# The second part's first norm is taken out of the start: its sums go behind the first head's token products, its scaling and shift beside the first group's queries

## The reference, cut to what matters

```python
mod = silu(c) @ w_ada + b_ada
sh1, sc1, g1, sh2, sc2, g2 = split(mod, 6)
hn = rmsnorm(x, norm1_w) * (1.0 + sc1) + sh1      # the "first norm"
proj = hn @ w_in                                  # q, k, v, gates, ...
...                                               # retention, RG-LRU, gates -> merged
x = x + g1 * (merged @ w_out)
hn2 = rmsnorm(x, norm2_w) * (1.0 + sc2) + sh2
x = x + g2 * peer(hn2, ...)                       # queries, top-k, experts gathered by token
y = rmsnorm(x, final_norm_w)
```

## Time and profile before

| | |
|---|---|
| median of 3 runs | 3748.63 us (3748.52 to 3752.19) |
| the profiled execution | 3746.89 us |
| its span, first to last instruction | 3745.1 us |
| PE busy | 3125.7 us (83%) |
| DVE busy | 2968.1 us (79%) |
| POOL busy | 1932.0 us (52%) |
| ACT busy | 1273.7 us (34%) |
| moved by DMA | 1126.16 MB |

### The profile page before, as it was taken

One profiled execution on the slowest core, in us unless ns is written; L12 is line 12 of the kernel. 1 busy time (PEld: TensorE's weight loads), 2 busy tenths in 40 slices (PEclk: granted clock), 3 DMA queues, 4 the chain that ended last, 5 costly groups with the idle time before them and its releaser, 6 DMA issues.

```text
span 3745.1 us, 56383 instructions
## 1 busy us (share of the span) xinstructions
PE 3125.7 (83%) x17498; PEld 2479.7 (66%) x17498; DVE 2968.1 (79%) x6226; ACT 1273.7 (34%) x2928; POOL 1932.0 (52%) x1504
## 2 busy tenths in 40 slices
PE   7999999989899999878999999899899999960100
PEld 4777776656666668767878788788777888850000
DVE  3444357998888877898899999899998876679898
ACT  3222211121222221686555555555545650000000
POOL 0000014444454553445667676667666756777676
PEclk9999999999999999999999999999999999985555
DMA  7444354666777787778999999999999999999998
GB/s 257 135 139 140 118 168 149 213 215 209 230 252 258 259 305 267 248 250 316 401 375 397 385 376 379 345 383 396 346 380 362 409 405 402 410 386 358 346 355 305
DMA packets 435094, 1126.16 MB, mean 301 GB/s; under 512 B 41856, under 2 KB 174336, under 8 KB 434944
## 3 DMA queue, kind: packets, MB, share of 16 engines
q0 software_dynamic: 204800, 745.10, 54.0%
q1 hardware_dynamic: 225376, 369.46, 27.9%
q10 hardware_dynamic: 4768, 9.96, 0.7%
HBM read 1098.29 MB, written 26.10 MB: 300 GB/s over the span
## 4 chain that ended last, share of the span: by engine, by line
PE 33%; DVE 24%; issue 15%; DMA 11%; POOL 3%; ACT 1%; DVEq 0%; ACTq 0%; POOLq 0%; SPq 0%
PE vacc L2264 12%; DVE rows L1679 9%; PE vacc L858 7%; DMA rows<-in_peer_u,eidx 7%; PE scat L2198 3%; POOL rows L1476 3%; PE vacc L829 3%; DVE oh1w L1758 2%; DMA rows<-in_peer_v,eidx 2%; DMA rows<-in_peer_v,g1T 2%; PE vacc L2178 1%; PE scat L2251 1%; DVE eidf L1571 1%; DVE htok L1689 1%; DVE hot L1665 1%
## 5 line engine op out<-in xcount | busy, mean ns | idle before, releaser
L1476 POOL DMA_INDIRECT rows<-in_peer_u,eidx x1088 | 1411.7, 1298 | 1070.1 <-DVE dots L1679 691.6
L1679 DVE CUSTOM_DVE_ANT_0 rows<-rows,htok 128x1024 f32<-128x1024 f32 x1088 | 1353.1, 1271 | 131.1 <-DMA rows<-in_peer_u,eidx 120.2
L2264 PE MATMUL vacc<-W,vbuf 128*128 (+1 forms) x6144 | 1427.9, 388 | 31.0 <-DMA vbuf<-in_peer_v 19.8
L2264 PEld LDWEIGHTS vacc<-W,vbuf 128*128 128x128 f32 x6144 | 1158.3, 193 | 182.4 <-issue 32.5
L2013 ACT ACTIVATE oh<-iota,e2s 128x128 bf16<-128x128 f32 x1536 | 486.5, 391 | 17.2 <-DVE wpart L1729 10.1
L858 PE MATMUL vacc<-W 128*128 128x384 f32 x1280 | 436.5, 497 | 1.2 <-ACTq L759 1.2
L1460 POOL TENSOR_TENSOR hot<-hot,cid 128x864 f32<-128x864 f32 x68 | 129.3, 1906 | 585.8 <-DVE hot L1665 584.6
L1689 DVE SCALAR_TENSOR_TENSOR htok<-rows,dots,htok 128x1024 f32<-128x1024 f32 x256 | 328.9, 1285 | 39.8 <-DMA rows<-in_peer_v,eidx 32.4
L858 PEld LDWEIGHTS vacc<-W 128*128 128x128 f32 x1280 | 243.5, 194 | 169.0 <-issue 10.8
L1476 POOL DMA_INDIRECT rows<-in_peer_v,eidx x256 | 286.8, 1120 | 100.4 <-issue 78.6
L2020 ACT ACTIVATE W<-scat 128x256 f32 (+1 forms) x320 | 122.6, 383 | 583.9 <-PE scat L2251 515.2
(11 more groups left out here) (327 smaller groups left out, 3089.4 us busy)
## 6 DMA issues: line engine op xcount, KB each, us to landing
vbuf<-in_peer_v SPq DMA_DIRECT2D x384, 512.0 KB
W<-in_w_in SPq DMA_DIRECT2D x80, 512.0 KB, 6.8
W<-in_wq SPq DMA_DIRECT2D x64, 512.0 KB
vbuf<-in_w_ada SPq DMA_DIRECT2D x9, 2048.0 KB, 8.2
rows<-in_peer_u,eidx POOLq DMA_INDIRECT x1088
W<-in_w_in SPq DMA_DIRECT2D x16, 1024.0 KB, 5.7
W<-in_w_ada SPq DMA_DIRECT2D x3, 2048.0 KB, 15.9
W<-in_w_out SPq DMA_DIRECT2D x12, 512.0 KB, 8.3
```

The lines of the kernel that those rows point to most:

```text
L1476: g.indirect_dma_start(rows[:, s, :], None, table[:, :], bass.IndirectOffsetOnAxis(ap=picked, axis=0)).then_inc(landed[s], 16)
L1679: v.tensor_tensor_reduce(rows[:, s, :], rows[:, s, :], htok[:, at % 2, :], 1.0, 0.0, ALU.mult, ALU.add, dots_of(t)[:, c:c + 1]).then_inc(u ...
L2264: mm = pe.matmul(vacc[:, k, :], vbuf[:, s, k * P:(k + 1) * P], W[:, e1, :].rearrange("p o t -> p (o t)"), start=(clear and s == 0 and k % ...
```

## The change

It does the following.

- SP's order in block 1: the load of B's `x` goes from behind the second slab to behind the eleven small tables, and the tables go from the end to just behind `w_qkv`. `wab`, the five `w_part`, S0 and the late slab come after these. The list of loads is the same.
- B's squares, sums and roots leave block 1. In block 2 ACT does the squares after `tokens_low` of the first head and then the two roots; PE does the sums after `qkv_low` of the first head, before `mix_tensor`.
- The inversion of `rstdB` goes from DVE's start of block 2 to its end, where also the shift's columns are copied to a new tile `sh1`.
- The 8 scalings of `hnB` go to DVE in block 3, behind `scale(0)`.
- The 8 shifts of `hnB` go to ACT in block 3, into the hook of `cross(0)`: one after each query copy from the ninth to the sixteenth. Each adds to a new semaphore `hnB_ready`, and PE waits for all 8 before B's first token products.
- The semaphore `fold_ready` is merged into `ones_ready`.

```diff
@@ block 1, SP
                 ada_load(1)
-                sp.dma_start(hnB, I["xT"][:, TA:T]...).then_inc(x_in[1], 16)
                 ada_load(2)
                 ada_load(3)
                 w_in_load(sp, 0, 0)
+                sp.wait_ge(act_done, 1)
+                for dst, src in ((rope_c, "rope_c"), (rope_s, "rope_s"), (dmask, "dmask"), (smask, "smask"), (xi, "xi"),
+                                 (zeta, "zeta"), (szeta, "szeta"), (gch, "gch"), (h0, "h0"), (c0, "c0"), (iota, "iota")):
+                    sp.dma_start(dst[:], I[src]).then_inc(small_in, 16)
+                sp.dma_start(hnB, I["xT"][:, TA:T]...).then_inc(x_in[1], 16)
                 sp.wait_ge(ones_ready, 4)
                 wab_load(sp, 0)
                 for j in range(1, 6):
                     w_in_load(sp, 0, j)
-                sp.wait_ge(act_done, 1)
-                for dst, src in (the same eleven):
-                    sp.dma_start(dst[:], I[src]).then_inc(small_in, 16)
                 s0_load(sp, 0)
                 sp.wait_ge(mod_ps, len(EARLY))
                 slab_load(sp, 0)
@@ block 1, ACT
                 copy_row(0)
                 copy_row(1)
-                squares(hnB, LATER, KC)
-                act.wait_ge(ssum_ready, 2)
-                act.activation(rstdB[:, 0:CUT], nps[:, 0:CUT], ACT.Sqrt, ...).then_inc(sd_ready, 1)
-                act.activation(rstdB[:, CUT:LATER], tps[:, 0:CUT], ACT.Sqrt, ...).then_inc(sd_ready, 1)
                 copy_row(2)
                 copy_row(3)
@@ block 1, PE
                 turn(1)
-                sums(zB, KC)
                 slab(2)
@@ block 2, ACT
                 act.wait_ge(small_in, 240)
-                for k in range(KC):
-                    act.wait_ge(scaled, KC + k + 1)
-                    act.activation(hnB[:, k, :], hnB[:, k, :], ACT.Identity, bias=modT[:, SH1 + k, 0:1])
                 tokens_high(act, zA, 0)
                 tokens_low(act, zA, 0)
+                squares(act, hnB, LATER, KC)
+                act.wait_ge(ssum_ready, 2)
+                act.activation(rstdB[:, 0:CUT], nps[:, 0:CUT], ACT.Sqrt, ...).then_inc(sd_ready, 1)
+                act.activation(rstdB[:, CUT:LATER], tps[:, 0:CUT], ACT.Sqrt, ...).then_inc(sd_ready, 1)
@@ block 2, PE
                 qkv_low(pe, zA, 0)
+                sums(pe, zB, KC)
                 with pe.Fori(0, H - 1) as f:
                     mix_tensor(pe, zA, f, False)
@@ block 2, DVE
-                v.wait_ge(sd_ready, 3)
-                dl_(v.reciprocal(rstdB, rstdB))
-                for k in range(KC):
-                    v.scalar_tensor_tensor(hnB[:, k, :], hnB[:, k, :], gain[:, k, 0:1], rstdB, ALU.mult, ALU.mult).then_inc(scaled, 1)
...
                 dl_.end(H)
+                v.wait_ge(sd_ready, 3)
+                dl_(v.reciprocal(rstdB, rstdB))
+                v.tensor_copy(sh1[:, :], modT[:, SH1:SH1 + KC, 0])
                 v.wait_ge(st_free, zA.nst * H)
@@ block 3, DVE
                 scale(0)
+                for k in range(KC):
+                    v.scalar_tensor_tensor(hnB[:, k, :], hnB[:, k, :], gain[:, k, 0:1], rstdB, ALU.mult, ALU.mult).then_inc(scaled, 1)
@@ block 3, ACT
-                cross(0, lambda x: None)
+                def second_half(x):
+
+                    if x >= KC:
+                        act.wait_ge(scaled, x + 1)
+                        act.activation(hnB[:, x - KC, :], hnB[:, x - KC, :], ACT.Identity, bias=sh1[:, x - KC:x - KC + 1]).then_inc(hnB_ready, 1)
+                cross(0, second_half)
@@ block 3, PE
                 pe.wait_ge(qh_ready, 16)
+                pe.wait_ge(hnB_ready, KC)
                 qkv_high(pe, zB, 0)
```

More of the change, by code:

```diff
@@ L366, in program @@
         ada_in = [sem(f"ada_in{i}") for i in range(len(EARLY))]
-        scaled = sem("scaled")
+        scaled, hnB_ready = sem("scaled"), sem("hnB_ready")
         def w_in_load(sp, f, j):
@@ L417, in slab_columns, with squares, sums @@
             return mm
+        def squares(act, x, n, lo):
+            act.wait_ge(x_in[lo // KC], 16)
+            for k in range(KC):
+                if lo + k >= 2:
+                    act.wait_ge(sq_used, lo + k - 1)
+                act.activation(sq[k % 2][:, 0:n], x[:, k, 0:n], ACT.Square).then_inc(sq_ready, 1)
+        def sums(pe, z, lo):
+            for k in range(KC):
+                pe.wait_ge(sq_ready, lo + k + 1)
+                for n, (a, b) in enumerate(z.slices):
+                    dst = pslice(z, pj, n) if z.sample else (nps, tps)[n][:, 0:CUT]
+                    mm = pe.matmul(dst, ones[:, :], sq[k % 2][:, a:b], start=(k == 0), stop=(k == KC - 1))
+                mm.then_inc(sq_used, 1)
+            pe.wait_ge(sq_used, lo + KC)
+            pe.sem_inc(ssum_ready, 1)
         with nc.Block() as block:
@@ L470, in copy_row @@
                     act.activation(row[u], R[u][0:ROWS, 0:ADA_W], ACT.Copy).then_inc(row_ready, 1)
-                squares(hnA, TA, 0)
+                squares(act, hnA, TA, 0)
                 act.wait_ge(ones_ready, 4)
@@ L491, in _ @@
                 pe.wait_ge(act_done, 1)
-                def sums(z, lo):
-                    for k in range(KC):
[L496 to L502, removed]
                 def slab(i):
@@ L519, in turn @@
                     slab_columns(pe, pk, u * 512, row[u]).then_inc(row_turned, 1)
-                sums(zA, 0)
-                pe.wait_ge(fold_ready, 3)
+                sums(pe, zA, 0)
+                pe.wait_ge(ones_ready, 7)
                 slab(0)
@@ L1203, in _ @@
                 act.wait_ge(small_in, 240)
-                for k in range(KC):
-                    act.wait_ge(scaled, KC + k + 1)
-                    act.activation(hnB[:, k, :], hnB[:, k, :], ACT.Identity, bias=modT[:, SH1 + k, 0:1])
                 tokens_high(act, zA, 0)
                 tokens_low(act, zA, 0)
+                squares(act, hnB, LATER, KC)
+                act.wait_ge(ssum_ready, 2)
+                act.activation(rstdB[:, 0:CUT], nps[:, 0:CUT], ACT.Sqrt, bias=epsb[:, 0:1], scale=1.0 / D).then_inc(sd_ready, 1)
+                act.activation(rstdB[:, CUT:LATER], tps[:, 0:CUT], ACT.Sqrt, bias=epsb[:, 0:1], scale=1.0 / D).then_inc(sd_ready, 1)
                 with act.Fori(0, H - 1) as f:
```

19 lines of the change are left out of this document (5 added, 14 removed).

## The result

| | before | after |
|---|---|---|
| median of 8 runs, beside one another | 3748.57 us (3747.58 to 3752.19) | 3760.64 us (3759.12 to 3769.69) |
| ratio of the runs | | 1.0035 [1.0026, 1.0044] |
| the profiled execution, its span | 3746.89, 3745.1 us | 3761.73, 3759.9 us |

The change makes the kernel 12.1 us slower, 0.35%, and the interval excludes no change. The prediction said slower, by 9.0, at 3757.6. The windows of the kernel after come first (stretch, length, busy us and count of PE, PEld, DVE, ACT and POOL, granted clock, DMA share, GB/s).

A forecast was written before the change was run, and what follows sets the result against it. Block 1 was taken as bound by SP's issuing, part A's mixing by PE. Terms: +10.5 (sums on PE) - 1.5 (SP sooner) + 0 + 0 = +9.0 us, predicting 3757.6, range 3750 to 3764.

The forecast's parts named there:

- Block 1 bound by SP: Block 1: it lasts as long as SP needs to issue its loads; removing sums and squares there is worth nothing.
- SP's end, -1.5: End of block 1: the new load order lets SP finish 1.5 us earlier, between -1 and 3.
- how many bytes were out: Block 1: about 0.4 MB of loads still untransferred when rope_c's issue ended at 48.40 us.
- twelve quick issues: SP's tail in block 1, called the tables: twelve issues in 6.81 us, moved to where SP is held anyway.
- The sums on PE, +10.5: Start of block 2: B's sums ahead of mix_tensor delay it 10.5 us, uncovered; bounds 9.8 and 20.8.
- the rival of the lower clock: Start of block 2: sums run at half clock, 10 us more, 3768; chance 0.07.
- The gain from the shift that went: Start of block 2: removing ACT's shift saves part of PE's 1.65 us wait, already counted in the 10.5.
- The end of block 2, 0: DVE's added reciprocal and copy make it 5.2 us later, still 3.1 before PE, so hidden.
- Block 3, 0: Scalings hidden in DVE's 14.22 us wait, shifts beside PE: cost 0, between 0 and 1; rival not hidden, chance 0.05.
- Carrying to the end: After block 3's start: waits are relative, so the delay is carried to the kernel's end.

The follow-up runs named there:

- e4: Changed kernel with SP's wab, five w_part, S0 and late slab issued at the head of block 2: 3744.98 us against 3746.16 before, 0.9994.
- e10: Changed kernel repeated unaltered on another chip: 3760.29 us against 3747.97 for the kernel before, 1.0040.
- e11: Changed kernel with block 1's old load order, second time, on another chip: 3763.10 us against 3747.97 before, 1.0039.
- e1: Kernel before with only B's inversion, scaling and shift moved late, as in the change: 3746.09 us against 3746.16, 1.0001.
- e2: Kernel before with 16 unused 128x384 matmuls added on PE where the change puts the sums: 3754.20 us against 3746.16, 1.0021.
- e3: Changed kernel with block 1's old load order, first time: 3758.83 us against 3746.16 for the kernel before, 1.0037.
- e9: Kernel before with late scaling and shift of B, DVE's scalings also waiting for PE's first query: 3745.01 us against 3749.31, one run.
- e12: Kernel before with 8 unused DVE operations added behind scale(0) in block 3: 3749.35 us against 3748.69, one run.
- e8: Changed kernel, most late loads at block 2's head, x of B last, B's squares and sums in PE's block 3 waits: 3733.97 us against 3749.31, 0.9958.
- e6: Kernel before, tables behind w_qkv, SP's tail at block 2's head, late scaling and shift of B: 3741.92 us against 3749.31, 0.9984.
- e13: Repeat of e6 against the kernel before: 3745.92 us against 3748.69, one run.

## Why the prediction was right or wrong

**Block 1 bound by SP: right, shown.** Taking squares, sums and slabs forward moved ACT's end by 12.6 us and SP's by 0.2; taking SP's tail out moved block 2 by 15 (e4).

**SP's end, -1.5: wrong.** This is the term of the sum that failed. Measured at the start of block 2 are -0.20 between the profiles of before and after, and +0.89 on one chip (e10, e11); no profile of the new order shows a gain near 1.5. The old order's block 2 starts at 55.2 to 55.7 in five profiles (e1, e2, e3, e9, e11), at 56.26 and 56.81 in two (before, e12); the new order's at 56.06 and 56.12. The failing assumption was that the table issues are free where SP is held, and that the transfers keep the 391 GB/s of the earlier trace rows up to the end. In fact the hold moved with the transfers: wab and the five w_part took 3.57 + 15.94 = 19.5 us to issue, 15.7 before, and S0 1.48 instead of 0.63. And the rate was not kept. It dips at 36 to 38 us (188 GB/s, 179 in e10, and 377 to 379 with the old order), which by 48 us had cost nothing, 340 GB/s on average against 338; and it falls off at the end, 221 at 50 to 54. By 54 us 329 GB/s had been moved on average (330 in e10) against 337, 0.43 MB less, which is 1.1 us at the assumed rate. Why the rate falls was not tried. Besides, the base was off by chance: rope_c's 3.13 in the earlier trace rows was 1.6 to 1.7 us in all six other profiles with the old order. One row of one execution carried the estimate of how many bytes were out. Two slips in the working didn't change the term: what moves forward are the eleven tables, while S0 and the late slab, counted among the "twelve quick issues", stay at the tail; and the loads up to x of B are 15.8 MB in the new order, not 17.

**The sums on PE, +10.5: right, somewhat small.** mix_tensor came 12.79 us behind the products' end, by the working 12.15. Of the missing 0.64, 0.17 is ahead of the first square, 0.27 the first matmul of the stretch and the pace, 0.20 the wait for the last sum (0.50, not 0.30). The pace of 1.29 us per k held (72.76 to 74.05), and the clock was full, so the rival of the lower clock had no place here. The gain from the shift that went, 0.9 us, was in the difference as stated (e1: 0.85).

**The end of block 2, 0: right.** DVE ended 3.25 before PE, predicted 3.1.

**Block 3, 0: right in its mechanism, +1.4 in the profile.** The scalings lay in DVE's wait: 14.22 less their 7.51, and 1.4 more since the scores came later, make the 8.19 that were left, within 0.1. The shifts did not hold up B's products, which come 75.1 us behind the first scores and came 75.3 behind them before. e1 shows no cost at the end. The queries' 1.4 us at the lower clock were no term of the sum. Whether they reach the end is not shown: the table falls from +11.74 to +10.50 by the expert keys, and stretches of single profiles scatter by as much.

**Carrying to the end: right, within the scatter.** +10.5 at 1740 us, +7.3 in e10; from there on the gather stage scatters by up to 11 us by itself, about as much as this change is worth, and only medians can decide. They say +12.1 and, on another chip, +12.3 (e10). The sum with the measured terms is -0.2 (or +0.9) + 11.1 + 0 + 0 = 10.9 to 12.0, beside +12.07 of the medians. So the forecast was right by its mechanism, the sums on PE, and its two errors did not cancel: both made it too low.

## What to carry to other kernels

Work taken out of a block that another queue bounds was worth nothing there (12.6 us on ACT's side, 0.2 on SP's), and cost its full time where it was put ahead of the engine that bounds the next block. Before moving work, find out what would have to go with it: here SP's last issues, after which the same work costs nearly the same up to mix_tensor in either place. If it must move, look for a stretch where its own engine waits, as e8 did. Don't count on a gain from reordering a queue of loads because some issues are short: in the two orders tried here the end of the queue stayed within about 1 us, for the hold came back at other issues.

## What the runs showed of the hardware

- How long an issue on SP took had little to do with its own size: the 3 MB of x of B took 0.43 us in the kernel after, at 32.58, and one w_part of 0.5 MB took 7.40 there, at 37.92. The same x of B took 4.95 in the kernel before, at 5.37, and the fourth slab (2 MB) 10.04, at 14.16. Short issues do not mean that nothing is under way: ten small tables were issued in 0.43 to 0.60 us each from 27.03 to 32.54, while 376 GB/s were moved (24 to 32).
- After the same wait of 5.4 us, PE's granted clock stayed at 0.50 for about 3 us in some kernels and 6 in others, the same both times in each of the three kernels that were profiled twice (after and e10, e3 and e11 long; e6 and e13 short), and not by DVE's work alone. It is worth 1.4 us. With PE kept in work before (e8) it was full from the first query.
- A slab's 16 matmuls of 128x512 took 1.90 us at the full clock and 3.60 at half of it. The fourth slab took 1.90 in the kernel after, behind a wait of 2.11, and 3.60 in e4, behind a wait of 1.85; in e10, the kernel after once more, it took 2.52. The wait just before does not tell which.
- Gathering the experts took 1997.6 to 2008.9 us in 14 profiles of code that is the same in this stage.
